# A two-layer decoder step on one core: six more page buffers for values, two places for split weights, gate weights first, another last LayerNorm

## The chip, the cores and the metric

The kernel runs on one core of a Trainium2 chip. The metric is the device time of one execution in microseconds, the median of three runs before: 950.03 us. PE is the matrix engine (TensorE), DVE the vector engine, ACT the scalar engine, POOL GpSimd, and SP the engine whose queue issues nearly all loads.

## The reference

One step for 256 prompt tokens and 64 sample tokens (8 sequences of 8) together, 1024 wide, all in float32. Layer one is a matrix-memory mixer (mLSTM), layer two reads a paged key and value cache: for each sequence 8 pages of 128 tokens of keys, and 8 of values, found through a page table. Both layers have a squared-ReLU MLP of 4096, and each half of a layer ends in a LayerNorm of x * ALPHA + h.

```python
def trunk(x, ...):
    for layer in range(DEPTH):
        if layer < N_A_LAYERS:
            h, state = mlstm_mixer(x, w_in_a[layer], b_gate_a[layer], w_out_a[layer], C0[layer], n0[layer], m0[layer])
        else:
            kv = x @ w_kv
            ctx = kv_side(k, v)
            q = (x @ w_q_b[j]).reshape(B, L, H_B, HD_B)
            h = attend(q, ctx).reshape(B, L, QB_W) @ w_out_b[j]
        x = layer_norm(ALPHA * x + h, ln_g[layer, 0], ln_b[layer, 0])
        x = layer_norm(ALPHA * x + sq_relu_mlp(x, w_up[layer], w_down[layer]), ln_g[layer, 1], ln_b[layer, 1])
```

## The kernel before

All activations lie turned, features on partitions: x is eight chunks of 128 features by 320 tokens. Each dense product is made of tiles of 128 output columns, 192 tiles in 24 groups of eight ("quads": query and key of the mixer, its output gate, its values, its output weights, eight quads of MLP, then the attention's query Q_WQ, keys Q_WK, values Q_WV, output Q_WOB, and eight quads of MLP). To keep float32 accuracy each operand is split into a high and a low part, and a tile is 24 matmuls (eight chunks, three products; lines 528 to 530), some 3.5 us of PE. ACT makes the high part of the weights (`split`, line 1015), DVE the low part (line 1389); both go to four places each, `w_hi` and `w_lo`, tile t to place t % 4, so ACT waits until tile t - 4 is done. Raw weights come in units of two tiles (1 MB) to four buffers; while pages are about, two of these four hold pages.

SP's queue is in order, and its program (lines 420 to 509) is written out by hand: loads of units, of pages, and the waits between them. A wait in it holds everything behind it. `load_page` sends page g to ring buffer g % 8 once page g - 8 has been used (`s_used`); numbers 0 to 63 are keys and 64 to 127 values. `load_unit` waits until both low splits of the unit that was in its buffer are made.

Keys: 32 pairs of pages; PE turns each page (line 845), ACT and DVE copy it, PE forms the scores of a pair (line 887), and between pairs stand the eight tiles of Q_WK and the turning of their results. Values: for two groups of four sequences, 32 pages each (line 939), with one tile of Q_WV before every fourth page of the first group, and the prompt's attention (`p_step`) between those of the second. Then the attention's output is rounded and the output tiles begin.

The start: the sample tokens come in two halves and the gate weights after them on ACT's queue (lines 1029, 1030); seventeen matmuls of zeros (line 561) run before PE turns the eight chunks of x, and the gates' matmuls (`gates`, lines 552 to 554) begin after the sixth chunk. DVE then makes low splits of three tiles and the gates' row chain (lines 1426 to 1447).

The end: after each of the last quad's tiles its chunk of x is final (line 1693), PE turns it back to tokens (`y_turn`), and DVE takes statistics (line 1638) and multiplies by the gain (`y_gained`). After the last, DVE joins the statistics (line 1909), ACT and DVE form 1/std, and DVE makes the result of three groups of tokens (128, 128, 64) by two long operations each (lines 1921, 1923); each group is stored as it is ready.

Of the kernel before, what the change touches and what calls it, by code (L numbers as in the profile page):

```python
# [12 lines left out]
F32 = mybir.dt.float32  # L13
# [6 lines left out]
DM = 1024  # L20
# [22 lines left out]
RAW, SPL = 4, 4  # L43

# [89 lines left out]
def build(nc, x_prompt, x_sample, state_C, state_n, state_m, cache_k, cache_v, page_table,  # L134
# [4 lines left out]
    with ctx:  # L139
# [16 lines left out]
        raw = [put(f"raw{i}", [128, 8, 256]) for i in range(RAW)]  # L156
        WH = [put(f"w_hi{i}", [128, 8, 128], F32R) for i in range(SPL)]
        WL = [put(f"w_lo{i}", [128, 8, 128], F32R) for i in range(SPL)]
# [88 lines left out]
        page = [put(f"page{i}", [128, DM], F32, w_) for i, w_ in enumerate([b_] * 4 + [raw_at] * 4)]  # L247
# [18 lines left out]
        st = put("y_stats", [128, 3, 8, 6], F32, fin_at)  # L266
        mv = put("y_mean_var", [128, 3, 2], F32, fin_at)
        fin = put("y_small", [128, 4, 3], F32, fin_at)
        evc, vc, rsc, nmr = [fin[:, i, :] for i in range(4)]
        QZ = [put("q_padded0", [128, H, 4, 32], F32, b_)]  # L270
# [49 lines left out]
        s_evr, s_evt, s_gbr = sem("eps_row_done"), sem("eps_turned"), sem("gain_bias_rows_in")  # L320
        s_vm, s_aqz, s_cq, s_cqc = [
# [10 lines left out]
        s_in = [sem(f"page_in{i}") for i in range(RING)]  # L332
# [87 lines left out]
        def _(sp):  # L420
# [73 lines left out]
            pages(NPG + 19, NPG + 28)  # L494
            load_unit(4 * Q_WOB + 1)
            pages(NPG + 28, 2 * NPG)
# [1497 lines left out]
```

## Time and profile before

| | us |
|---|---|
| median of three runs | 950.03 (949.31 to 952.37) |
| the profiled execution | 950.97 |
| its span, first to last instruction | 949.2 |
| PE busy | 914.6 (96%) |
| DVE busy | 632.2 (67%) |
| ACT busy | 430.1 (45%) |
| mean granted clock of PE | 0.984 of full |
| HBM read and written | 175.22 MB, 6.32 MB |

A row of the profile gives an engine, the line of the kernel, the operation with its output and input, and times. Idle time stands with what released the engine. In the chain of waits each row is a start, a length and what ran or was waited for, followed back from the last instruction; it is the view that says what a saving would be worth. "Windows" gives the busy time of each engine in a stretch, with the clock that PE was granted.

### The profile page before, as it was taken

How to read it: one execution, taken by the hardware profiler on the slowest of the kernel's cores; microseconds unless marked ns; L12 is line 12 of the kernel's file. 1: busy time of each engine (PE TensorE's matmuls, PEld its weight loads, DVE VectorE, ACT ScalarE, POOL GpSimd, SP SyncE). 2: the span in 40 equal slices, each digit the busy share in tenths (PEclk: the TensorE clock that was granted, in tenths of full speed). 3: DMA queues.
4: the chain of work that ended last, by engine and by line, in shares of the span. 5: the costliest groups of instructions: out<-in, count | busy, mean ns of one | idle time of the engine just before them, and what ended most of it. 6: DMA issues, size and time to landing. Idle time of an engine off the chain costs nothing.

```text
span 949.2 us, 18902 instructions
## 1 busy us (share of the span) xinstructions
PE 914.6 (96%) x7571; PEld 855.8 (90%) x7571; DVE 632.2 (67%) x1117; ACT 430.1 (45%) x806; POOL 56.3 (6%) x69
## 2 busy tenths in 40 slices
PE   8999998999999999999999999989899999999993
PEld 7999977989999999999888778877799999999993
DVE  4667568868887475677576847435468797747556
ACT  3435563457446254445344453333446644526320
POOL 0000006400000000220000000000130000000000
PEclk8999999999999999999999999999899999999997
DMA  9953313654454454465887998999654445554401
GB/s 284 268 172 103 121 45 82 180 167 161 134 166 146 137 171 137 146 246 186 311 280 253 349 360 308 385 391 394 188 174 134 143 142 204 149 161 133 135 1 55
DMA packets 134075, 182.77 MB, mean 193 GB/s; under 512 B 5827, under 2 KB 116107, under 8 KB 133988
## 3 DMA queue, kind: packets, MB, share of 16 engines
q1 hardware_dynamic: 125994, 175.97, 56.1%
q10 hardware_dynamic: 7354, 3.49, 1.4%
q0 software_dynamic: 640, 2.10, 0.8%
q8 instruction: 60, 0.98, 0.4%
q14 instruction: 27, 0.22, 0.1%
HBM read 175.22 MB, written 6.32 MB: 191 GB/s over the span
## 4 chain that ended last, share of the span: by engine, by line
PE 88%; DVE 5%; ACT 2%; DMA 2%; issue 1%; ACTq 1%; SPq 0%; DVEq 0%
PE ps L528 23%; PE ps L530 23%; PE ps L529 23%; PE ps L845 6%; PE ps L887 3%; PE ps L939 2%; DMA page<-in_cache_v_dram 1%; DVE w_lo L1389 1%; DMA wg_raw<-in_w_in_a_dram 1%; PE ps L543 1%; ACTq L1135 0%; PE ps L714 0%; DVE y_tok L1923 0%; ACT probs_turned L1316 0%; PE ps L924 0%
## 5 line engine op out<-in xcount | busy, mean ns | idle before, releaser
L1015 ACT ACTIVATE w_hi<-raw 128x1024 fp32r<-128x1024 f32 x192 | 202.6, 1057 | 251.9 <-PE ps L530 249.4
L1389 DVE TENSOR_TENSOR w_lo<-raw,w_hi 128x1024 fp32r<-128x1024 f32 x192 | 235.1, 1225 | 112.9 <-ACT w_hi L1015 112.6
L528 PE MATMUL ps<-x_hi,w_hi 128*128 128x322 f32 (+1 forms) x888 | 279.8, 315 | 0.4 <-DVE w_lo L1389 0.4
L530 PE MATMUL ps<-x_hi,w_lo 128*128 128x322 f32 (+1 forms) x888 | 276.6, 312 | 0.0
L529 PE MATMUL ps<-x_lo,w_hi 128*128 128x322 f32 (+1 forms) x888 | 276.1, 311 | 0.0
L528 PE MATMUL ps<-h_hi,w_hi 128*128 128x320 f32 x640 | 200.7, 314 | 2.0 <-DVE h_lo L1897 1.1
L529 PE MATMUL ps<-h_lo,w_hi 128*128 128x320 f32 x640 | 199.1, 311 | 0.0
L530 PE MATMUL ps<-h_hi,w_lo 128*128 128x320 f32 x640 | 198.9, 311 | 0.0
L528 PEld LDWEIGHTS ps<-x_hi,w_hi 128*128 128x128 f32 x888 | 168.3, 189 | 6.0 <-ACT k_turned L1282 2.9
L529 PEld LDWEIGHTS ps<-x_lo,w_hi 128*128 128x128 f32 x888 | 168.7, 190 | 0.2
L530 PEld LDWEIGHTS ps<-x_hi,w_lo 128*128 128x128 f32 x888 | 167.6, 189 | 0.0
L528 PEld LDWEIGHTS ps<-h_hi,w_hi 128*128 128x128 f32 x640 | 121.6, 190 | 6.2 <-DVE x L1552 3.4
L529 PEld LDWEIGHTS ps<-h_lo,w_hi 128*128 128x128 f32 x640 | 121.6, 190 | 0.0
L530 PEld LDWEIGHTS ps<-h_hi,w_lo 128*128 128x128 f32 x640 | 121.5, 190 | 0.0
L845 PE MATMUL ps<-base,page 128*128 128x128 f32 x512 | 63.3, 275 | 0.7 <-ACT k_turned L1282 0.7
L845 PEld LDWEIGHTS ps<-base,page 128*128 128x128 f32 x512 | 56.3, 141 | 8.0 <-issue 6.2
L1756 DVE COPY k_turned<-ps 128x512 f32<-128x512 f32 x64 | 43.8, 690 | 24.6 <-PE ps L845 23.4
L1693 DVE TENSOR_TENSOR x<-x,ps 128x320 f32<-128x320 f32 x64 | 31.1, 487 | 42.3 <-PE ps L530 41.2
L1282 ACT ACTIVATE k_turned<-ps 128x512 f32<-128x512 f32 x64 | 36.1, 591 | 28.0 <-PE ps L845 28.0
L1666 DVE SCALAR_TENSOR_TENSOR fm<-ln_neg_mu,ps 128x320 f32<-128x320 f32 x64 | 35.0, 547 | 3.8 <-PE ps L530 3.7
L1668 DVE SCALAR_TENSOR_TENSOR fm<-ln_std,ps,fm 128x320 f32<-128x320 f32 x64 | 35.6, 556 | 2.3
L939 PE MATMUL ps<-page,probs_turned 128*32 128x128 f32 x1024 | 33.4, 275 | 3.6 <-DMA page<-in_cache_v_dram 2.0
(330 smaller groups left out, 884.7 us busy)
## 6 DMA issues: line engine op xcount, KB each, us to landing
raw<-in_w_up_dram SPq DMA_DIRECT2D x32, 1024.0 KB, 5.7
raw<-in_w_down_dram SPq DMA_DIRECT2D x32, 1024.0 KB, 5.3
page<-in_cache_k_dram SPq DMA_DIRECT2D x64, 512.0 KB, 5.2
page<-in_cache_v_dram SPq DMA_DIRECT2D x64, 512.0 KB, 7.2
raw<-in_w_in_a_dram SPq DMA_DIRECT2D x12, 1024.0 KB, 9.2
raw<-in_w_kv_dram SPq DMA_DIRECT2D x8, 1024.0 KB, 6.5
raw<-in_w_out_a_dram SPq DMA_DIRECT2D x4, 1024.0 KB, 5.3
raw<-in_w_q_b_dram SPq DMA_DIRECT2D x4, 1024.0 KB, 5.2
```

Of the source, the lines that this page charges most:

```text
L528: mm(out, WH[t % SPL][:, k, :], hi[:, k, 0:width], start=(k == 0), stop=False)
L529: mm(out, WH[t % SPL][:, k, :], lo[:, k, 0:width], start=False, stop=False)
L530: last = mm(out, WL[t % SPL][:, k, :], hi[:, k, 0:width], start=False, stop=(k == 7))
L845: last = nc.tensor.transpose(bank[:, 128 * j:128 * j + 128], page[P % RING][:, 128 * h:128 * h + 128], ident)
L939: last = mm(o_bank(G, bb)[32 * j:32 * j + 32, c:c + 128], PT[G][:, 8 * a_ + p, 32 * j:32 * j + 32], page[g % RING][:, 128 * h:128 * h + 12 ...
L1015: A(WH[t % SPL][:, :, :], raw[RBUF[u]][:, :, 128 * (t % 2):128 * (t % 2) + 128], ACT.Copy)\
L1282: A(KT[P // 2 % 2][:, 0:4, 128 * (P % 2):128 * (P % 2) + 128], slot_bank(P // 2, 2 * (P % 2))[:, :].rearrange("p (h t) -> p h t", h=4), AC ...
L1389: V.tensor_tensor(WL[t % SPL][:, :, :], raw[RBUF[t // 2]][:, :, 128 * (t % 2):128 * (t % 2) + 128], WH[t % SPL][:, :, :].bitcast(F32), ALU ...
L1666: own(V.scalar_tensor_tensor(f[:, :], nmu[:, :], bank[:, T:T + 1], bank[:, 0:T], ALU.mult, ALU.add))
L1668: V.scalar_tensor_tensor(f[:, :], sd[:, :], bank[:, T + 1:TW], f[:, :], ALU.mult, ALU.add)\
L1693: V.tensor_tensor(X[:, n, :], X[:, n, :], bank[:, 0:T], ALU.add)\
L1756: V.tensor_copy(KT[P // 2 % 2][:, 4:8, 128 * (P % 2):128 * (P % 2) + 128], slot_bank(P // 2, 2 * (P % 2) + 1)[:, :].rearrange("p (h t) -> ...
```

## The change

- Value pages 0 to 5 get buffers of their own, `page8` to `page13`: four in places 2 and 3 of `w_hi` and `w_lo`, one over the squares and sums of the LayerNorm, one over the padded queries of the first group. They are loaded between the key pages. After that all fourteen buffers take values in turn, from value page 50 on only ten.
- While pages are about, split weights of Q_WK and Q_WV have places 0 and 1 only (`PLACE`), and a tile's splits are made after the evacuation of the tile two before, in place of ahead of it. Units and pages change their order in SP's queue, and SP waits there for "all query tiles done", and for pair 15's scores before value page 5.
- The gate weights are issued ahead of the sample tokens on ACT's queue; nineteen warming matmuls, not seventeen. DVE splits tile 3 within the row chain.
- The last LayerNorm: y_turn stands within the next tile, ahead of its fifth chunk; DVE's statistics and gain of a chunk come before the next residual; seven chunks' statistics are joined ahead of the last tile. The sample tokens leave DVE's long operations: ACT makes gained rows of each chunk, PE turns them by a matmul with the identity, and at the end adds (-mean, std) times (gain, bias) to them; ACT scales by 1/std and stores. The second prompt group is finished and stored in two halves.

```diff
+PLACE = [t % 2 if Q_WK <= t // 8 <= Q_WV else t % SPL for t in range(NT)]
+PLACE_BEFORE = [max((w for w in range(t) if PLACE[w] == PLACE[t]), default=-1) for t in range(NT)]
...
+EARLY, LEFT_OUT = 6, 50
+PAGE_AT = [g % RING for g in range(NPG)]
+_turn = [RING + i for i in range(EARLY)] + list(range(RING))
+for _v in range(NPG):
+    if _v == LEFT_OUT:
+        _turn = [b for b in _turn if not RING <= b < RING + 4]
+    PAGE_AT.append(_turn[0])
+    _turn = _turn[1:] + _turn[:1]
+PAGE_BEFORE = [max((w for w in range(g) if PAGE_AT[w] == PAGE_AT[g]), default=-1) for g in range(2 * NPG)]
+PAGE_LOADS = [PAGE_AT[:g + 1].count(PAGE_AT[g]) for g in range(2 * NPG)]
+PLACES_FREE = max(g for g in range(2 * NPG) if RING <= PAGE_AT[g] < RING + 4) + 1
...
-page = [put(f"page{i}", [128, DM], F32, w_) for i, w_ in enumerate([b_] * 4 + [raw_at] * 4)]
+sq_at = [fs_at]
+page = [put(f"page{i}", [128, DM], F32, w_)
+        for i, w_ in enumerate([b_] * 4 + [raw_at] * 4 + [wh_at] * 2 + [wl_at] * 2 + [sq_at])]
...
-        if g >= RING:
-            sp.wait_ge(s_used, g - RING + 1)
-        sp.dma_start(page[g % RING][:, :], cache[bass.ds(number, 1)].rearrange("a t h d -> (a t) (h d)"))\
-            .then_inc(s_in[g % RING], 16)
+        if PAGE_BEFORE[g] >= 0:
+            sp.wait_ge(s_used, PAGE_BEFORE[g] + 1)
+        sp.dma_start(page[PAGE_AT[g]][:, :], cache[bass.ds(number, 1)].rearrange("a t h d -> (a t) (h d)"))\
+            .then_inc(s_in[PAGE_AT[g]], 16)
...
+    sp.wait_ge(s_mm, 8 * Q_WQ + 8)
+    pages(8, 12)
+    load_page(NPG)
+    pages(12, 16)
+    load_page(NPG + 1)
+    pages(16, 18)
     load_unit(4 * Q_WK + 3)
-    pages(8, 22)
+    pages(18, 21)
+    load_page(NPG + 2)
+    pages(21, 24)
+    load_page(NPG + 3)
+    pages(24, 26)
     load_unit(4 * Q_WV)
-    pages(22, 30)
+    pages(26, 30)
+    load_page(NPG + 4)
+    pages(30, 34)
     load_unit(4 * Q_WV + 1)
-    pages(30, 40)
+    pages(34, 37)
+    sp.wait_ge(s_sc, 16)
+    load_page(NPG + 5)
+    pages(37, 42)
     load_unit(4 * Q_WV + 2)
-    pages(40, NPG + 9)
+    pages(42, NPG)
+    pages(NPG + EARLY, NPG + 17)
     load_unit(4 * Q_WV + 3)
-    pages(NPG + 9, NPG + 19)
+    pages(NPG + 17, NPG + 27)
     load_unit(4 * Q_WOB)
-    pages(NPG + 19, NPG + 28)
+    pages(NPG + 27, NPG + 36)
     load_unit(4 * Q_WOB + 1)
-    pages(NPG + 28, 2 * NPG)
+    pages(NPG + 36, 2 * NPG)
...
+        sp.dma_start(gb2[i:i + 1, :], row[1, 1:2, :]).then_inc(s_gbr, 16)
...
+    sp.wait_ge(s_yf, 1)
+    sp.dma_start(y_prompt[0, 0:128, :], Yt[:, 0, :]).then_inc(s_yp, 16)
...
-        sp.wait_ge(s_yf, i + 1)
-        sp.dma_start(y_prompt[0, 128 * i:128 * i + 128, :], Yt[:, i, :]).then_inc(s_yp, 16)
-    sp.wait_ge(s_yp, 16 * 2)
+        sp.wait_ge(s_yf, i + 2)
+        c = slice(512 * i, 512 * i + 512)
+        sp.dma_start(y_prompt[0, 128:256, c], Yt[:, 1, c]).then_inc(s_yp, 16)
+    sp.wait_ge(s_yp, 16 * 3)
...
-    for i in range(17):
+    for i in range(19):
...
-        if n >= 4:
-            pe.wait_ge(s_ty, n - 3)
-        turn3(ps[2 + n % 4], X[:, n, :]).then_inc(s_yt, 1)
+        if n >= 2:
+            pe.wait_ge(s_ty, n - 1)
+        turn3(ps[2 + n % 2], X[:, n, :]).then_inc(s_yt, 1)
+        pe.wait_ge(s_xg, n + 1)
+        mm(ps[4 + n // 4][0:64, 128 * (n % 4):128 * (n % 4) + 128], XG[:, n, :], ident, start=(n % 4 == 0),
+           stop=True, skip_group_check=True)
...
+    def y_between(n, t):
...
+        def ready(k):
+            if k == 4:
+                y_turn(n - 1)
+            return s_lo, t + 1
+        return ready
...
+    def y_sample_centred():
...
+        pe.wait_ge(s_msd, 1)
+        pe.wait_ge(s_ty, 8)
+        nc.tensor.transpose(ps[2][0:2, 0:64], ms[:, :], ident[0:64, 0:64]).then_inc(s_mst, 1)
+        pe.wait_ge(s_msc, 1)
+        pe.wait_ge(s_gbr, 64)
+        for half in range(2):
+            mm(ps[4 + half][0:64, :], msT[:, :], gb2[:, 512 * half:512 * half + 512], start=False, stop=True,
+               skip_group_check=True).then_inc(s_yz, 1)
...
-                    dense(t, HH[g % 2], HL[g % 2])
+                    dense(t, HH[g % 2], HL[g % 2], y_between(n, t) if l == 2 and i == 7 and n >= 1 else None)
...
-                if l == 2 and i == 7 and n >= 1:
-                    y_turn(n - 1)
...
-        if t >= SPL:
-            act.wait_ge(s_mm, t - SPL + 1)
-        A(WH[t % SPL][:, :, :], raw[RBUF[u]][:, :, 128 * (t % 2):128 * (t % 2) + 128], ACT.Copy)\
+        if PLACE_BEFORE[t] >= 0:
+            act.wait_ge(s_mm, PLACE_BEFORE[t] + 1)
+        if t == 8 * Q_WOB + 2:
+            act.wait_ge(s_used, PLACES_FREE)
+        A(WH[PLACE[t]][:, :, :], raw[RBUF[u]][:, :, 128 * (t % 2):128 * (t % 2) + 128], ACT.Copy)\
...
+    act.dma_start(wgraw[:, :, :], lhs_k(win[:, 3072:3088])).then_inc(s_gw, 16)
...
-    act.dma_start(wgraw[:, :, :], lhs_k(win[:, 3072:3088])).then_inc(s_gw, 16)
...
+                    if i == 7 and l == 2:
+                        act.wait_ge(s_xr, 8 * 3 + n + 1)
+                        A(XG[:, n, :], X[:, n, TP:T], ACT.Copy, scale=lnT[:, 24 + n:25 + n]).then_inc(s_xg, 1)
...
-        split_to(t + 4)
+        split_to(min(t + 4, 8 * Q_WK + 1))
...
-        split_to(8 * Q_WV + n + 3)
...
+        split_to(8 * Q_WV + n + 2)
...
-    act.wait_ge(s_yf, 3)
+    act.wait_ge(s_mst, 1)
+    A(msT[:, :], ps[2][0:2, 0:64], ACT.Copy).then_inc(s_msc, 1)
+    for half in range(2):
+        act.wait_ge(s_yz, half + 1)
+        A(Yt[0:64, 2, 512 * half:512 * half + 512], ps[4 + half][0:64, :], ACT.Copy, scale=rsc[0:64, 2:3])\
+            .then_inc(s_yc, 1)
+    act.wait_ge(s_yc, 2)
...
+    split(3)
...
-            ins = V.bn_stats(st[0:w, i, n, :], ps[2 + n % 4][0:w, 128 * i:128 * i + 128])
-        if n == 7:
+            ins = V.bn_stats(st[0:w, i, n, :] if n < 7 else st8[0:w, i, 3:9],
+                             ps[2 + n % 2][0:w, 128 * i:128 * i + 128])
+        if n >= 6:
...
-        bank, c = ps[2 + n % 4], slice(128 * n, 128 * n + 128)
+        bank, c = ps[2 + n % 2], slice(128 * n, 128 * n + 128)
...
-            dve.wait_ge(s_gbr, 32)
+            dve.wait_ge(s_gbr, 64)
...
-                        bcast(gbR[:, 0, c], 1, 2), ALU.mult)
-        V.tensor_tensor(Yt[0:64, 2, c], bank[0:64, 256:384], gbR[0:64, 0, c], ALU.mult).then_inc(s_ty, 1)
+                        bcast(gbR[:, 0, c], 1, 2), ALU.mult).then_inc(s_ty, 1)
...
+    def y_joined():
...
+        for i, w in ((0, 128), (1, 128), (2, 64)):
+            ins = V.bn_aggr(mv[0:w, i, :], st[0:w, i, :, :].rearrange("p n s -> p (n s)"))
+        own(ins)
+        V.tensor_copy(st8[:, :, 1], mv[:, :, 0])
+        V.tensor_scalar(st8[:, :, 2], mv[:, :, 1], 896.0, None, ALU.mult)
...
+                        V.memset(st8[:, :, 0:1], 896.0)
...
+                    if i == 7 and l == 2 and n >= 1:
+                        split_to(t + 3)
+                        y_stats(n - 1)
+                        y_gained(n - 1)
+                        if n == 7:
+                            y_joined()
...
+    split_to(8 * Q_WOB + 3)
...
-        ins = V.bn_aggr(mv[0:w, i, :], st[0:w, i, :, :].rearrange("p n s -> p (n s)"))
+        ins = V.bn_aggr(mv[0:w, i, :], st8[0:w, i, :])
...
+    V.tensor_scalar(ms[:, 0:1], mv[0:64, 2, 0:1], -1.0, None, ALU.mult)
...
+    V.tensor_tensor(ms[:, 1:2], vc[0:64, 2:3], rsc[0:64, 2:3], ALU.mult).then_inc(s_msd, 1)
...
-    for i, w in ((0, 128), (1, 128), (2, 64)):
-        if i == 2:
-            dve.wait_ge(s_yf, 1)
-        own(V.scalar_tensor_tensor(YZ[i % 2][0:w, :], gbR[0:w, 0, :], nmr[0:w, i:i + 1], gbR[0:w, 1, :],
+    for i in range(2):
+        own(V.scalar_tensor_tensor(YZ[i][:, :], gbR[:, 0, :], nmr[:, i:i + 1], gbR[:, 1, :],
...
-        V.scalar_tensor_tensor(Yt[0:w, i, :], Yt[0:w, i, :], rsc[0:w, i:i + 1], YZ[i % 2][0:w, :],
-                               ALU.mult, ALU.add).then_inc(s_yf, 1)
+        for c in ((slice(0, DM),), (slice(0, 512), slice(512, DM)))[i]:
+            V.scalar_tensor_tensor(Yt[:, i, c], Yt[:, i, c], rsc[:, i:i + 1], YZ[i][:, c],
+                                   ALU.mult, ALU.add).then_inc(s_yf, 1)
```

## Rows read from the trace of the kernel before

**Rows 1.** The page: PE busy us, share, count; DMA share in 40 slices

```profile
PE 914.6 (96%) x7571; PEld 855.8 (90%) x7571; DVE 632.2 (67%) x1117; ACT 430.1 (45%) x806; POOL 56.3 (6%) x69
...
DMA  9953313654454454465887998999654445554401
```

**Rows 2.** Chain of waits, 0 to 85 us: start us, us, what

```profile
2.03 7.39 DMA wg_raw<-in_w_in_a_dram
...
12.87 0.27 PE ps L553
...
16.78 0.44 ACT x_hi L1038
...
30.94 0.15 PE ps L529
```

**Rows 3.** DMA issues before 2.1 us: size, us from issue to landing

```profile
x_tok<-in_x_sample_dram ACTq DMA_DIRECT2D x1, 128.0 KB, 3.0
...
x_tok<-in_x_sample_dram ACTq DMA_DIRECT2D x1, 128.0 KB, 4.5
...
wg_raw<-in_w_in_a_dram ACTq DMA_DIRECT2D x1, 64.0 KB, 7.4
```

**Rows 4.** PE's timeline, 9 to 50 us: start, us, operation, [idle before <-releaser]

```profile
11.46 0.61 PE L552 MATMUL ps<-x_hi,wg_hi 128*128 128x320 f32 x1 [1.46 <-DVE wg_lo L1415]
...
30.12 0.39 PE L528 MATMUL ps<-x_hi,w_hi 128*128 128x320 f32 x1 [0.41 <-DVE w_lo L1389]
```

**Rows 5.** Windows: us, busy PE PEld DVE ACT POOL, clock, DMA share, GB/s

```profile
11.50:17.30 5.80, 5.80 (x20) 4.82 (x21) 2.39 (x7) 1.91 (x6) 0.14 (x1) 0.50 1.08 361
```

**Rows 6.** Timeline of DVE, 9 to 40 us

```profile
18.20 3.50 DVE L1389 TENSOR_TENSOR w_lo<-raw,w_hi 128x1024 fp32r<-128x1024 f32 x3
...
24.26 0.48 DVE L1430 SCALAR_TENSOR_TENSOR row<-row,row 8x320 f32<-8x320 f32 x1 [1.04 <-ACT row L1046]
```

**Rows 7.** The chain of waits, 520 to 538 us

```profile
520.21 1.00 PE ps L887 x16
...
528.37 1.75 PE ps L845 x16
...
537.36 1.90 PE ps L845 x16
```

**Rows 8.** DMA view of 525:530, 590:600 and 610:615

```profile
page<-in_cache_k_dram SPq DMA_DIRECT2D x3, 512.0 KB, 4.4
...
DMA packets 1736, 3.63 MB, mean 363 GB/s; under 512 B 92, under 2 KB 1108, under 8 KB 1733
...
page<-in_cache_v_dram SPq DMA_DIRECT2D x5, 512.0 KB, 8.6
```

**Rows 9.** Windows as in rows 5: the keys' end, the values' middle

```profile
530.00:568.00 38.00, 38.00 (x450) 28.53 (x448) 22.70 (x42) 20.23 (x48) 0.00 (x0) 1.00 0.96 354
...
605.00:617.00 12.00, 10.75 (x165) 9.87 (x167) 5.72 (x12) 4.09 (x12) 0.00 (x0) 1.00 1.04 396
```

**Rows 10.** PE's waits, 568 to 674 us: total us, times, longest

```profile
PE ps L939 <- DMA page<-in_cache_v_dram: 2.0, 2, 1.3
```

**Rows 11.** Values, 583 us in the chain of waits, 617 us in PE's timeline

```profile
583.48 1.88 PE ps L939 x64
...
616.89 0.65 PE L939 MATMUL ps<-page,probs_turned 128*32 128x128 f32 x16 [1.25 <-DMA page<-in_cache_v_dram]
```

**Rows 12.** The chain of waits, 700 to 710 us: one 320-column pair

```profile
706.19 0.54 PE ps L750 x2
```

**Rows 13.** Timeline of DVE, 930 to 950 us

```profile
933.64 0.49 DVE L1693 TENSOR_TENSOR x<-x,ps 128x320 f32<-128x320 f32 x1 [2.25 <-PE ps L530]
...
935.88 0.82 DVE L1909 BATCH_NORM_AGGREGATE y_mean_var<-y_stats 128x2 f32<-128x48 f32 x3
...
938.20 1.28 DVE L1921 SCALAR_TENSOR_TENSOR y_rest<-gain_bias_rows,y_small 128x1024 f32<-128x1024 f32 x1
...
944.55 1.28 DVE L1923 SCALAR_TENSOR_TENSOR y_tok<-y_tok,y_small,y_rest 64x1024 f32<-64x1024 f32 x1
```

More of the change, by code:

```diff
@@ L265, in build @@
         gbR = put("gain_bias_rows", [128, 2, DM], F32, gb_at)
-        st = put("y_stats", [128, 3, 8, 6], F32, fin_at)
+        st = put("y_stats", [128, 3, 7, 6], F32, fin_at)
+        st8 = put("y_stats_joined", [128, 3, 9], F32, fin_at)
         mv = put("y_mean_var", [128, 3, 2], F32, fin_at)
         fin = put("y_small", [128, 4, 3], F32, fin_at)
+        XG = put("x_sample_gained", [128, NC8, TS], F32, fin_at)
+        ms = put("y_mean_std", [64, 2], F32, fin_at)
+        msT = put("y_mean_std_rows", [2, 64], F32, fin_at)
+        assert fin_at[0] <= b_[0] + 4096
+        gb2 = put("gain_bias_pair", [2, DM], F32, h1_at)
         evc, vc, rsc, nmr = [fin[:, i, :] for i in range(4)]
+        qz_at = [b_[0]]
+        page.append(put("page13", [128, DM], F32, qz_at))
         QZ = [put("q_padded0", [128, H, 4, 32], F32, b_)]
@@ L320, in build @@
         s_evr, s_evt, s_gbr = sem("eps_row_done"), sem("eps_turned"), sem("gain_bias_rows_in")
+        s_xg, s_msd, s_mst, s_msc, s_yz = [
+            sem(n) for n in ("x_sample_gained", "y_mean_std_done", "y_mean_std_turned", "y_mean_std_copied",
+                             "y_sample_centred")]
+        s_yc = sem("y_sample_done")
         s_vm, s_aqz, s_cq, s_cqc = [
@@ L331, in build @@
             sem(n) for n in ("pS_done", "p_max", "p_exp", "p_norm", "p_turn", "p_turn_copied", "p_out", "p_out_copied")]
-        s_in = [sem(f"page_in{i}") for i in range(RING)]
+        s_in = [sem(f"page_in{i}") for i in range(RING + EARLY)]
         s_used, s_half = sem("page_used"), sem("page_half_turned")
@@ L527, in dense @@
                         pe.wait_ge(*chunk_ready(k))
-                    mm(out, WH[t % SPL][:, k, :], hi[:, k, 0:width], start=(k == 0), stop=False)
-                    mm(out, WH[t % SPL][:, k, :], lo[:, k, 0:width], start=False, stop=False)
-                    last = mm(out, WL[t % SPL][:, k, :], hi[:, k, 0:width], start=False, stop=(k == 7))
+                    mm(out, WH[PLACE[t]][:, k, :], hi[:, k, 0:width], start=(k == 0), stop=False)
+                    mm(out, WH[PLACE[t]][:, k, :], lo[:, k, 0:width], start=False, stop=False)
+                    last = mm(out, WL[PLACE[t]][:, k, :], hi[:, k, 0:width], start=False, stop=(k == 7))
                 last.then_inc(s_mm, 1)
@@ L845, in turn_page @@
                         last = nc.tensor.transpose(bank[:, 128 * j:128 * j + 128],
-                                                   page[P % RING][:, 128 * h:128 * h + 128], ident)
+                                                   page[PAGE_AT[P]][:, 128 * h:128 * h + 128], ident)
                     last.then_inc((s_half, s_used)[half], 1)
@@ L940, in page_values @@
                                   PT[G][:, 8 * a_ + p, 32 * j:32 * j + 32],
-                                  page[g % RING][:, 128 * h:128 * h + 128],
+                                  page[PAGE_AT[g]][:, 128 * h:128 * h + 128],
                                   start=(bb % 2 == 0 and p == 0 and a_ == 0), stop=True, skip_group_check=True)
@@ L998, in _ @@
             y_turn(7)
+            y_sample_centred()
         @block.scalar
@@ L1388, in split @@
                 dve.wait_ge(s_hi, t + 1)
-                V.tensor_tensor(WL[t % SPL][:, :, :], raw[RBUF[t // 2]][:, :, 128 * (t % 2):128 * (t % 2) + 128],
-                                WH[t % SPL][:, :, :].bitcast(F32), ALU.subtract).then_inc(s_lo, 1)
+                V.tensor_tensor(WL[PLACE[t]][:, :, :], raw[RBUF[t // 2]][:, :, 128 * (t % 2):128 * (t % 2) + 128],
+                                WH[PLACE[t]][:, :, :].bitcast(F32), ALU.subtract).then_inc(s_lo, 1)
                 split_upto[0] = t + 1
@@ L1449, in _ @@
             for n in range(8):
-                split(8 * Q_QK + n + 3)
+                split_to(8 * Q_QK + n + 3)
                 if n < 5:
@@ L1701, in mlp @@
                             split_to(t + 4)
-                            if i == 7 and l == 2 and n >= 1:
-                                y_stats(n - 1)
-                                y_gained(n - 1)
             mlp(0, Q_MLP0, 8)
@@ L1872, in _ @@
                 kvq(16 + n)
+                split_to(8 * Q_WV + n + 2)
                 if n == 0:
```

13 lines of the change are left out of this document (7 added, 6 removed).

## The prediction

> **What bounds the kernel now.** I read the page's first two parts, then the chain of waits, then PE's own waits, then the windows of three places. PE is busy 96% of the span, and the chain that ended last lies on PE for 88% of it; the DMA engines are full only at the start and in slices 21 to 29 [rows 1]. So nothing is to be had in the weight tiles as such: a change helps only where PE waits, runs at the low clock, or has ended. There are three such places. (a) The first 17 us: the chain waits 7.39 us for the gate weights, then PE turns and multiplies at a granted clock of 0.50, which is the 1.2 GHz level [rows 2, 5]. (b) The stretch of value pages, 573 to 667 us: PE's wait for pages is only 2.0 us in all, in two pieces [rows 10], though DMA there is full at 396 GB/s [rows 9]. (c) The end: VectorE's chain from the last residual at 933.64 to 945.83 us [rows 13].
>
> **Part (a), the gate weights first.** Before, three transfers stand on ACT's queue: the sample tokens' two halves, landing 3.0 and 4.5 us after their issue at 0.75 and 1.38 us, and then the gate weights, issued at 2.03 and landing 7.4 us later, at 9.42 [rows 2, 3]. ACT waits for them before it rounds x, so the first gate matmul stands at 11.46, and PE has idled since 10.0; its clock then is 0.50 until 17.3 [rows 4, 5]. A gate matmul takes 0.27 us of the chain at the low level, one of the same size 0.15 at the high one [rows 2]. After the second sample half was in (1.38 + 4.5 = 5.9), the weights took 3.5 us more, although they are many small pieces. Issued first, with data flowing from about 2.0 us, they should land between 2.0 + 3.5 = 5.5 and 2.0 + (9.4 - 3.3) = 8.1 us (3.3: issue 2.03 plus the same 1.3 us until data flows). The samples now queue behind them, at 6 to 8.6. I take the early end, because 3.5 us is what the weights took with half of the queue's company gone. The two more warming matmuls end at about 6.45 instead of 5.9 (0.28 each), so PE's turning starts 0.55 us later but runs into the gates with no idle time: six chunks to 10.4 us, gates from 10.4 instead of 11.46, at the high level. The twelve gate matmuls and two chunks between 11.46 and the last x_hi at 16.78 [rows 2] took 5.3 us, and at the high level take 12 x 0.15 + 2 x 0.57 = 2.9. That gives 1.1 + 2.4 = 3.5 us. Everything behind moves with it: the three low splits of 18.20 us [rows 6] start about 3.3 earlier, and their two raw units, issued at 3.37 and 6.43 and 9.3 and 9.2 us on the way, are just there. Splitting tile 3 inside VectorE's 1.04 us gap (it waits for ACT there [rows 6]) costs the row chain some 0.2 us, off PE's path, and takes away PE's 0.41 us wait at 30.12 [rows 4]. I take **-3.5 us**; ends -4.5 and +0.5 (the late end, where PE idles after warming and its clock starts low again).
>
> The Trainium skill, DMA: Bandwidth & Descriptors, section Queues, rings and completion order, says that on each DMA engine one queue's descriptors are consumed in ring order. By that rule the samples can land no earlier than about when the gate weights do, which speaks against this swap; the trace has them in that order (3.75, 5.9, 9.4 us), and the late end of the term is its price.
>
> **Part (b), keys.** Six value pages now go out among the keys, and the split weights of the K and V tiles have two places, not four. A high split must wait for the tile two before, not four: V tiles start 5.9 us apart, and the split weights of tile n+2 are ready 4.1 us after tile n ends, before it is wanted. PE loses nothing there. SP's queue is another matter, since it waits in two new ways. It stands at "pair 15 scored" (521.2 us [rows 7]) before it loads value page 5 and key page 37. Key 37 is then issued at 522.8 (SP issued pages each 1.1 us at 602 to 604) and lands 4.4 us later [rows 8], or 5.7 behind the value page: 527.2 to 528.5; it is read at 529.3, second of the pair at 528.37 [rows 7]. Then SP stands again, for the raw buffer of V's third unit: its release needs V tile 1 split into the one place that K tile 7 holds until 525.0, so about 529.5 to 530. Key 42 leaves at 531.4 behind 1 MB (2.6 us) and lands near 537; it is read at 537.36 [rows 7]. Behind it pages come each 1.3 to 1.45 us and are eaten each 1.45. Slack 0 to 0.5 us: I take **+0.5**, ends 0 and +2.5 (landings of 8.6 us as in the value stretch [rows 8]).
>
> **Part (b), values.** The six pages are a lead of 6 x 0.52 MB / 396 GB/s = 8 us of DMA. But the third place where SP stands eats it: V's fourth unit waits until V tile 3 is split, and that place is held until V tile 1 is done at 583.5 [rows 11]; with VectorE's and ACT's evacuation (1.7), the high (1.05) and low split (1.22) this is 587.6 us, and since SP is in order pages 17 and on wait too. From then 47 pages, 3 units and the stores, 29.1 MB, take 73.5 us at 396 GB/s: done at 590.5 + 73.5 = 664.0. Against PE's need: page 28 lands at 611.7 (it is read at 616.89, held by DMA 1.25 us [rows 11, 10]; without the holds it would be read at 614.6), the last at 664.0 for 664.7 (it was read at 666.7). So both holds go, with little to spare, and the tail (attention output, then dense) is PE's own and follows: **-1.7 us** (2.0 less 0.3 for thin places); ends -2.5 and +6.7, the latter at the 354 GB/s of the keys' end [rows 9]: 82 us.
>
> The same page of the skill, section Bandwidth, gives about 358 GB/s as the limit of one core for HBM transfers. That would make the last page 8 us later than PE wants it; the rows show 396 over 12 us of full load [rows 9], so the measurement decides for me, and 363 over a stretch that is not quite full [rows 8] keeps the chance alive.
>
> The splits of output tiles 2 and 3, now after ACT's last rounding, take 2 x 1.05 on ACT and 2 x 1.22 on VectorE; both end at about 676.6 of the old times, the residual wants VectorE at 678, the tile PE at 681: nothing, hidden under output tiles 0 and 1.
>
> **Part (c), the end.** Added on PE: eight matmuls of 128 columns for the sample rows, two instructions each. Their nearest row is the 320-column pair at 0.54 us [rows 12]: 0.22 each, seven of them before the last tile ends, 1.5 us; the turn of chunk 6, formerly behind the last tile, is now inside it: 0.33. VectorE's early joining of seven chunks (statistics 0.68, gain 0.40, aggregate 0.82, two small ones 0.2) may exceed the rest of the last tile by 0.2. So the last residual comes 2.0 us later. Then: statistics of chunk 7 come right behind its turn, -0.4; three aggregates over 9 elements instead of 48 (0.82 us [rows 13]) -0.5; two small operations +0.2; and of six long operations (1.21 to 1.28 each, 938.20 to 945.83 [rows 13]) four remain, one in halves: -2.5. Sum 2.0 - 0.4 - 0.5 + 0.2 - 2.5 = **-1.2 us**; ends -2.5 and +0.5. The sample rows go round by PE beside this: two products of 512 columns, 0.54 x 512/320 = 0.9 us each [rows 12], 1.8 at the low clock, and ACT's copies, 4.9 us in all from the factors on, as long as VectorE's four; it would be late by at most 0.5.
>
> **The sum.** -3.5 + 0.5 - 1.7 - 1.2 = -5.9 us against the profiled execution, 950.97 us (span 949.2, and 1.8 around it), which is 0.94 above the median of the three timed runs; the same difference off the median 950.03 gives **944.1**.
>
> **The rivals.** *The start gives nothing* (samples land late, PE's clock low again until about 15): then -2.4 in all, **947.6**. For it: the order on ACT's queue [rows 3]; against it: the 3.5 us that the weights took alone. *The lead is worthless*: SP's standing still leaves the two holds where they were and costs a microsecond at keys 37 and 42: -3.5 + 1 + 0 - 1.2, **946.3**. *Slower*: one mechanism, SP standing behind the split weights with only two places, in its two spots. If transfers after each standstill run at 354 GB/s and land after 8.6 us, key 37 and key 42 come 2.5 us late and the last value page 6.7 us late: -3.5 - 1.2 + 2.5 + 6.7 = +4.5, **954.5**. It decides from the point where the last value page lands more than 5 us after 664.7. *More than I think*: start -4.5, tail -2, values -2.5, keys 0: **941.0**.
>
> **How the numbers follow.** Forecast 0.50, no start 0.18, no lead 0.13, more 0.11, slower 0.08. The range leaves out half of the 941.0 case and the slow one, and takes in 947.6 with an upper bound from a half-lost start and late keys: 941.0 to 948.8. About 0.3% (2.85 us) is what a measurement of this kernel can tell from no change: below 947.2 is faster. The forecast, the no-lead and the more case lie there, and a third of the first rival: 0.80; same 0.13; slower 0.07.
>
> **What would show it.** In the changed profile: the first gate matmul near 10.4 at 0.15 us pace and a granted clock near 1 in the window 9 to 17; the sample halves landing by 6.5; PE's first waits on key pages at 37 and 42, under 0.5 us; SP's standstill from about 579 to 588 with DMA idle in it; no wait of PE for value pages; the last residual 2 us later against its tile, and the last VectorE operation 1.2 us earlier against the chain. Wrong if PE waits for value pages by more than 2 us, or if the low clock still covers the gates.

## The result: slower by 2.8%, and the profile after

The changed kernel takes 979.97 us (median of four runs, 978.0 to 983.25) against 951.2 for the one before (four runs, 949.31 to 957.9): a ratio of 1.0282, 95% interval 1.0236 to 1.0327. I had predicted 944.1. The kernel before scatters by itself: its 19 runs beside the first experiments lie between 944.4 and 959.0, so small effects are read below from stages of the profiles as well as from medians.

The page of the kernel after: busy us of each engine, then the granted clock in 40 slices, then the DMA queues (SP's is q1, ACT's q10).

```profile
PE 928.1 (95%) x7594; PEld 859.3 (88%) x7594; DVE 628.8 (64%) x1116; ACT 435.0 (44%) x817; POOL 56.3 (6%) x69
...
PEclk9999999999999999999989999988999999999998
...
q1 hardware_dynamic: 126142, 175.98, 54.4%
q10 hardware_dynamic: 7354, 3.49, 1.3%
```

PE is busy 13.5 us longer with nearly the same instructions [rows 1], because part of them ran at a lower clock, and it stands idle longer as well. To find where, I cut each profile at the same events: first turn of a key page, last score of a cached key, first product of a value page, first residual of the attention output (its dense tile done), last residual, end. All in us; the 3.3 us between keys and values are the same in every kernel and left out.

| profile | keys begin | keys | values, prompt attention | dense tiles | end | span |
|---|---|---|---|---|---|---|
| before | 443.3 | 126.5 | 104.9 | 255.6 | 15.6 | 949.2 |
| after | 437.9 | 148.9 | 114.9 | 259.8 | 13.0 | 977.8 |
| difference | -5.4 | +22.4 | +10.0 | +4.2 | -2.6 | +28.6 |

So the start gave more than forecast, the end about what was forecast, and two stages that I had at +0.5 and -1.7 cost 32 us. Where they lie is in PE's own waits of the kernel after: total us, times, longest.

```profile
PE ps L922 <- DVE k_turned L1859: 12.0, 13, 1.1
PE ps L887 <- DVE p_logit L1846: 9.7, 1, 9.7
...
PE ps L600 <- ACT k_turned L1365: 2.9, 8, 0.4
```

None of the three is among the waits of before at that size (there `p_logit` was 1.5 us, `k_turned` 0.7). None is a wait for a page, either: the value pages' 2.0 us [rows 10] are gone, and key pages cost PE 0.2 us. The first and third line are the keys: PE wants to turn the next page, and its PSUM bank is still being copied out. The windows of the whole key stage (us, then busy time of PE, PEld, DVE, ACT, POOL with counts, clock, DMA share, GB/s), before and after:

```profile
443.30:569.80 126.50, 125.84 (x1274) 100.71 (x1272) 82.60 (x145) 57.49 (x125) 0.00 (x0) 1.00 0.87 303
```

```profile
437.90:586.80 148.90, 133.14 (x1274) 102.86 (x1272) 82.16 (x145) 58.24 (x125) 0.00 (x0) 0.97 0.77 279
```

The same 1274 matmuls, and DVE and ACT have no more to do. PE idles 15.8 us instead of 0.7 (15.1 more) and is busy 7.3 us more, and together that is the 22.4. The 7.3 go with the clock, which is 0.97 on the mean of the stage instead of 1.00 and falls in single stretches with such gaps, for instance in this one:

```profile
494.00:500.00 6.00, 4.93 (x34) 3.24 (x33) 3.65 (x7) 0.96 (x2) 0.00 (x0) 0.72 0.99 355
```

### The profile page after: what moved, and what is told of

Read it like the earlier page. It is cut to its first block, busy times and chain, and to the rows that moved or that the text cites. A ratio compares the mean times of both kernels' runs of the same rounds, so it can differ in the third digit from the quotient of the medians.

```text
span 977.8 us, 18965 instructions
## 1 busy us (share of the span) xinstructions
PE 928.1 (95%) x7594; PEld 859.3 (88%) x7594; DVE 628.8 (64%) x1116; ACT 435.0 (44%) x817; POOL 56.3 (6%) x69
## 4 chain that ended last, share of the span: by engine, by line
PE 86%; DVE 6%; ACT 3%; issue 2%; ACTq 1%; DMA 1%; SPq 0%; DVEq 0%; POOL 0%; POOLq 0%
PE ps L585 23%; PE ps L587 22%; PE ps L586 22%; PE ps L922 4%; PE ps L964 3%; PE ps L1016 2%; ACTq L1215 1%; ACT w_hi L1095 1%; DMA page<-in_cache_k_dram 1%; DVE k_turned L1859 1%; DVE w_lo L1478 1%; PE ps L1001 1%; PE ps L618 1%; DVE kvq L1820 0%; DVE kvq L1819 0%
## 5 line engine op out<-in xcount | busy, mean ns | idle before, releaser
L922 PE MATMUL ps<-base,page 128*128 128x128 f32 x512 | 66.8, 283 | 12.8 <-DVE k_turned L1859 12.0
L922 PEld LDWEIGHTS ps<-base,page 128*128 128x128 f32 x512 | 57.9, 145 | 22.9 <-issue 20.7
L964 PE MATMUL ps<-k_turned,q_padded 128*32 128x256 f32 x512 | 36.0, 402 | 0.0
```

Of the source, the lines that this page charges most:

```text
L922: last = nc.tensor.transpose(bank[:, 128 * j:128 * j + 128], page[PAGE_AT[P]][:, 128 * h:128 * h + 128], ident)
L964: last = mm(ps[SCORE_BANK[2 * a_ + r // 2]][32 * j:32 * j + 32, 256 * (r % 2):256 * (r % 2) + 256], QZ[G][:, 4 * a_ + j, bb, :], KT[pair % ...
```

## Theories

*Mine, after the result.* The key stage pays for the **order on ACT and DVE**. With two places, the splits of tile n+2 cannot stand ahead of the evacuation of tile n, as those of n+3 did, without waiting for that tile's end: they were put behind it, and so ahead of the copies that free PE's banks. The values pay for something near the stores of `v_tok`. *Rivals:* SP's standstills starve PE of key pages; the transfers themselves got slower; two places as such are the cost, in whatever order. The experiments take one edit of the change at a time (the start, the end, the order), and then the stores.

## Experiments

**1. The start alone**, on the kernel before: two warming matmuls more, the gate weights first on ACT's queue, tile 3 split inside the gates' row chain.

```diff
-            for i in range(17):
+            for i in range(19):
...
+            act.dma_start(wgraw[:, :, :], lhs_k(win[:, 3072:3088])).then_inc(s_gw, 16)
             for i in range(2):
...
-            act.dma_start(wgraw[:, :, :], lhs_k(win[:, 3072:3088])).then_inc(s_gw, 16)
...
+            split(3)
             dve.wait_ge(s_gln, 1)
```

> The kernel before with the start of the change alone: gate weights first on ACT's queue, nineteen warming matmuls, tile 3 split within the row chain. The trace after shows the last query tile 5.4 us earlier than before. If that is the start's own and it carries through, this is 5 us faster than before: 944 to 946. Rival: the 5.4 us are given back at the key pages, whose loads are bound elsewhere: under 1 us gained.

Ratio 1.0004 [0.9967, 1.0041] (950.45 us, 10 runs), and not the 944 to 946 that I expected. In its profile the keys begin at 438.6, 4.7 us before those of the kernel before, but the value stage takes 113.2 us instead of 104.9. The gain of that profile is lost again by something else, near 622 us: ACT stands 10.23 us in issuing the stores of `v_tok`, and PE then waits 7.7 us for the prompt's attention. That is a first sign that the stores can go wrong without any of the six pages.

**2. The end alone**: the new last LayerNorm on the kernel before, with the sample rows' part taken through PE by an identity matmul for each tile.

> The kernel before with the new last LayerNorm alone. The trace after has 4.40 us a tile in the last quad where before has 3.85, and 13.0 us behind the last residual where before has 15.6. Theory: the matmul with the identity costs 0.55 us a tile, seven times 0.55 is more than the 2.6 us saved at the end: 1 to 2 us slower than before. Rival, my prediction's step at 0.22 us a matmul: 1.2 us faster.

Ratio 1.0021 [0.998, 1.0063] (951.28, 10 runs): the interval holds both no change and the 1 to 2 us of the expectation. Dense tiles 259.8 us instead of 255.6, end 12.5 instead of 15.6: +4.2 and -3.1. Its start is the old one, yet its keys begin at 439.2: before's own start has two forms. The windows of 11.50 to 17.30 us in this kernel and in the next one (old start too) show them:

```profile
11.50:17.30 5.80, 5.80 (x39) 5.42 (x38) 4.56 (x8) 4.35 (x6) 0.14 (x1) 1.00 1.08 362
```

```profile
11.50:17.30 5.80, 5.80 (x24) 4.86 (x23) 3.18 (x8) 2.76 (x7) 0.14 (x1) 0.56 1.08 361
```

With 1.07 us of idle time before the first gate matmul the clock stayed at 1.00 and PE got through 39 instructions; with 1.57 us it was granted 0.56, and 24 got through. Keys began at 439.2 and 445.0. Of the six profiles with the old start, two were at 1.00 there (experiment 2, and before in experiment 6) and four at 0.50 to 0.56 (before, and experiments 3, 5 and 8). The length of the idle time alone does not decide it. In experiment 5 the clock was low after only 0.75 us of it:

```profile
11.50:17.30 5.80, 5.80 (x23) 4.82 (x23) 2.34 (x6) 2.07 (x4) 0.14 (x1) 0.54 1.08 362
```

**3. The order alone**: the kernel before, with its four places, but the splits behind the evacuation, on ACT and on DVE.

```diff
-                    split_to(8 * Q_WK + n + 3)
                     kvq(8 + n)
+                    split_to(8 * Q_WK + n + 3)
```

> The kernel before, with four places for split weights and its own pages, but in the key pairs the split of the weights stands behind the evacuation of the key tile on ACT and on DVE, not ahead of it. Theory: the order makes the loss, since DVE then waits for ACT's split (ACT evacuates, 0.56, then splits, 1.05) before it copies turned keys, and PE waits for those banks: 15 to 22 us slower. Rival: two places make it, since a split has to wait for the tile two before: no change here, under 1 us.

Ratio 1.0196 [1.0112, 1.0279] (973.52, 4 runs). Keys 147.0 us against 126.5: this swap alone costs 20.5 us where the whole change costs 22.4, with no page moved and no place taken. Its waits of PE are those of after:

```profile
PE ps L845 <- DVE k_turned L1756: 11.1, 12, 1.1
...
PE ps L543 <- ACT k_turned L1282: 2.6, 7, 0.4
```

How it comes about is in the timeline of DVE in the kernel before, and then after, behind the same tile (start, us, operation, idle time before and releaser):

```profile
456.41 0.49 DVE L1717 TENSOR_TENSOR kvq<-kvq,ln_rstd 128x320 f32<-128x320 f32 x1
456.82 1.52 DVE L1756 COPY k_turned<-ps 128x512 f32<-128x512 f32 x2
```

```profile
450.79 0.49 DVE L1820 TENSOR_TENSOR kvq<-kvq,ln_rstd 128x320 f32<-128x320 f32 x1
452.86 1.23 DVE L1478 TENSOR_TENSOR w_lo<-raw,w_hi 128x1024 fp32r<-128x1024 f32 x1 [1.57 <-ACT w_hi L1095]
454.00 1.28 DVE L1859 COPY k_turned<-ps 128x512 f32<-128x512 f32 x2
```

Before, the copy follows the evacuation at once. After, DVE first waits 1.57 us for ACT, then splits for 1.23, and the copy comes 2.8 us later. ACT in the kernel after has the high split ahead of its own copies:

```profile
451.31 0.56 ACT L1319 ACTIVATE k_attn<-kvq,b_times_w 128x320 f32<-128x320 f32 x1 [5.78 <-DVE kvq L1820]
451.78 1.04 ACT L1095 ACTIVATE w_hi<-raw 128x1024 fp32r<-128x1024 f32 x1
452.73 1.06 ACT L1365 ACTIVATE k_turned<-ps 128x512 f32<-128x512 f32 x2
```

And PE pays at the banks (L600 turns the tile's K rows, L922 the next page):

```profile
453.36 0.33 PE L600 MATMUL ps<-base,k_attn 128*128 128x128 f32 x1 [0.37 <-ACT k_turned L1365]
...
454.83 1.94 PE L922 MATMUL ps<-base,page 128*128 128x128 f32 x16 [0.92 <-DVE k_turned L1859]
```

**4. After, with the splits one pair later** (behind `kv_out`, ahead of the odd pair's copies), two places and six pages kept.

```diff
                     kv_out(n)
+                    split_to(8 * Q_WK + n + 2)
                 else:
                     kvq(8 + n)
-                    split_to(8 * Q_WK + n + 2)
```

> The changed kernel with two places and all its pages, but the splits of the key tiles stand one pair later, behind the stores of the turned key tile, where no tile has just ended. If the order makes the loss the key stretch returns from 146.9 to 125 or 127 us and the whole to 958 to 961. Rivals: two places or SP's standing still make it: the key stretch stays above 135 us, the whole above 968.

Ratio 1.012 [1.0056, 1.0185] (964.68, 4 runs). Keys 132.6 instead of 148.9, clock 1.00: 16.3 of the 22.4 are back; I had expected nearly all (keys 125 to 127, the whole 958 to 961). Of the 6.1 left 3.2 are again copies, now at the dense tile's banks (7 waits of up to 0.5 us on ACT's `k_turned`); smaller waits make 2.1, 0.5 of them for key pages, and PE is busy 0.8 longer. Two places, six pages and SP's three standstills are all still in here, so in the key stage they cost 6.1 us at most in this order. Values stay bad, at 116.8: ACT stands 12.14 us at the stores.

**5. Two places in before's order**: the kernel before with the splits of n+2 ahead of the evacuation of n, where those of n+3 stood.

> The kernel before with two places for the split weights of key and value tiles and the unit loads set later in SP's order accordingly; no early pages; the splits stand ahead of the evacuation as in before. Order alone, with four places, took 147.0 us for the keys, before 126.5. Theory: with two places a split can't start before the tile two before has ended, which is when its evacuation is due, so the order of before doesn't save it: DVE waits for ACT's split first and evacuates later: 143 to 150 us. Rival: the order is all: 126 to 129 us.

One execution: 1014.0 us, keys 157.0 and values 137.0; before took 961.06 beside it and beside the single executions of experiments 7 and 8, so only the stages are read from these three. Here the rival is right in its own way: none of the three orders tried with two places (keys 148.9, 132.6 and 157.0) reaches the 126.5 of four. Ahead of the evacuation the split needs a place that PE frees only at the end of the very tile that is to be evacuated, and the evacuation stands behind it on ACT and DVE. PE waits for the evacuations, the first row in the values and the second in the keys:

```profile
PE ps L546 <- ACT fm L1239: 21.8, 8, 3.1
PE ps L848 <- DVE kvq L1720: 17.5, 8, 2.2
```

**6. The stores moved**, in before and in after: the three stores of `v_tok` leave ACT's queue, and SP issues them among the loads of the last MLP (`outs` keeps the count that the end waits for; SP's side is left out here).

```diff
-            for q in range(2):
-                store(p_v[0, 128 * q:128 * q + 128], VT[:, q, :, 0:128])
-            store(s_v_d.rearrange("b t h d -> (b t) h d"), VT[0:64, 2, :, 0:128])
+            outs[0] += 3
```

> The kernel before with the three stores of the new values issued by SP in the last MLP, where its queue has time, in place of by ACT between the values' last copy and the prompt attention. In the traces so far ACT stands at these stores for 4.0, 3.9 and 4.9 us (before, tail alone, order alone) or for 10.2, 12.1 and 12.1 us (start alone, changed kernel, splits one pair later), and PE then waits up to 9.7 us for the prompt attention. Theory: the stores' issue is what makes both the changed kernel's last 8 to 10 us and the spread of the kernel before (944 to 959): PE's 1.5 us wait goes and no run is above 950; median 1.5 to 5 us below before. Rival: the pages' own transfers hold the second half of the values: under 0.5 us.

> The changed kernel with the same three stores moved to SP in the last MLP. Theory: from the first value page to the first output residual it takes 104 to 106 us as in before, not 114.9: the whole 979 becomes 968 to 971. Rival: fourteen pages in flight slow PE's second half by themselves: under 3 us gained.

Before: 0.9973 [0.9951, 0.9995] (948.56, 12 runs; none above 951.1, where the 20 runs of before beside them, median 950.26, reach 956.9). After: 969.78 (4 runs), ratio to before 1.0203 [1.0166, 1.0241] in place of 1.0282. By the medians moving them gave 1.7 us in before and 10.2 in after (7.5 by the two ratios). I had expected no run of the former above 950 (three of the 12 are) and the latter at 968 to 971. The value stage is 101.6 and 102.1 us: 0.5 apart in place of 10.0, and both shorter than the 104.9 of before. So 9.5 of the +10.0 go with these stores. ACT's timeline around them, before and then after (ACTq is the issue of a DMA):

```profile
626.61 4.03 ACTq L1135 DMA_DIRECT2D out_dram<-v_tok  x2
630.69 0.40 ACT L1249 ACTIVATE p_logit<-p_logit,p_stats 128x128 f32<-128x128 f32 x1 [3.98 <-DVE p_stats L1736]
```

```profile
643.37 12.11 ACTq L1215 DMA_DIRECT2D out_dram<-v_tok  x2
655.52 0.40 ACT L1332 ACTIVATE p_logit<-p_logit,p_stats 128x128 f32<-128x128 f32 x1 [12.15 <-issue]
```

Behind the issue stands the first exponential of the prompt attention, and PE waits 9.7 us for what comes of it. In after the chain of waits passes through the last of these issues:

```profile
644.09 11.39 ACTq L1215
```

Behind that the clock is low. After, 643.4 to 655.5 and 656 to 670:

```profile
643.40:655.50 12.10, 4.23 (x88) 3.11 (x88) 1.16 (x3) 0.00 (x0) 0.00 (x0) 0.87 1.04 407
656.00:670.00 14.00, 12.66 (x183) 10.08 (x184) 5.08 (x19) 3.49 (x14) 0.00 (x0) 0.64 0.96 339
```

**7. A ring of eight from value page 14 on**, in the kernel after, to test one reason for the long issue: more pages under way at once than before, so that the stores find fuller queues.

```diff
-    if _v == LEFT_OUT:
-        _turn = [b for b in _turn if not RING <= b < RING + 4]
+    if _v == EARLY + RING:
+        _turn = [b for b in _turn if b < RING]
```

> The changed kernel, with its six early pages, but from value page 14 on only the eight old buffers take pages. ACT stood 12.1 us at the stores in both runs with fourteen buffers, 4 to 10 in those with eight. Theory: the number of page transfers under way sets how long the stores' issue lasts: 4 to 6 us here, and 107 to 110 us from the first value page to the first output residual in place of 114.9. Rival: it does not: 10 to 12 us again. The keys stay at 148 or 149 us.

One execution: 978.66 us, values 116.1, and the issue stood 11.05 us:

```profile
641.03 11.05 ACTq L1215 DMA_DIRECT2D out_dram<-v_tok  x2
```

So fourteen buffers at the time of the stores are not needed for a long issue, and experiment 1 says the same: eight buffers, and 10.23 us. But the profiles do sort by something in the change: with the six early pages ACT stood 12.11 (after), 12.14 (experiment 4) and 11.05 us, and with before's pages 4.03, 4.06, 4.94 and 3.60 (before, experiments 2, 3 and 8), 2.70 for all three stores in experiment 5, and 10.23 once (experiment 1).

**8. The identity matmuls left out** of the kernel of experiment 2. It leaves out the sample rows' x in their last LayerNorm.

> The new last LayerNorm alone, on the kernel before, with the eight matmuls with the identity left out (the sample rows come out wrong: their x is missing; the turns stay in the middle of the tiles). Tail alone took 259.8 us from the first output residual to the last residual, before 255.6. Theory: the identity matmul costs the 0.55 us a tile: 255.6 to 256.2 here. Rival: breaking a tile in two for the turn costs it: 258 to 260 here.

One execution, 948.91 us. Dense tiles 256.1 us instead of 259.8, end 13.1. The matmuls themselves are the cost; that the row of dense matmuls is broken there is not (it was broken before too, by the turns of x). What one costs is in the chain of the kernel after, against 0.15 for each dense matmul around it:

```profile
962.38 0.11 PE ps L602
962.48 0.36 PE ps L831 x2
962.85 0.34 PE ps L585
963.19 0.15 PE ps L586
```

0.36 for the two instructions and 0.34 - 0.15 = 0.19 for the dense matmul behind them: 0.55 us for each of the seven tiles that now hold one; the period from tile to tile grew from 3.85 to 4.40.

**9. Start and stores, and two early pages.** The start's edits with the moved stores; and the same with two value pages loaded ahead, in two buffers whose space is idle by then (the squares' and the padded q's), with four places for the split weights and before's order.

```diff
+PAGE_AT = [g % RING for g in range(NPG)]
+_turn = [RING, RING + 1] + list(range(RING))
+for _v in range(NPG):
+    PAGE_AT.append(_turn[_v % len(_turn)])
...
-            pages(22, 30)
+            pages(22, 26)
+            sp.wait_ge(s_mm, 8 * Q_WQ + 8)
+            load_page(NPG)
+            pages(26, 30)
```

> The kernel before with the start of the change and with the stores moved. Start alone reached its first key page 4.7 us earlier than before, and lost it at the stores (10.2 us). Theory: with the stores gone the start's gain is kept: 943 to 945. The start's gain in the low-clock case is 5 us, in a run where the clock stays high anyway (tail alone reached its keys at 439.2) about 1, so against the moved stores alone it is 1 to 5 us. Rival: the start is given back in another place: same as the moved stores alone.

> Like the run before it, plus two early value pages in the two buffers that cost no split weights (over the LayerNorm's squares and over the padded queries), ten buffers in turn for values; four places for split weights and the order of before. Theory: the keys stay at 126.5 us, PE's 2 us of waits for value pages go, yet PE's own chain hides most of it: 0 to 2 us faster than without. Rival of the change's idea: a lead of two pages, 2.6 us of transfer, is worth its 2 us in full or more.

946.2 us (9 runs, 943.93 to 947.52), ratio 0.9953 [0.9932, 0.9975], a little above the 943 to 945 expected; and **942.81** (6 runs, 941.03 to 945.17), ratio 0.991 [0.9884, 0.9936]. The second beats both kernels. Its keys take 126.6 us, as before, and PE's wait for value pages is 0.3 us in place of 2.0 in before and 2.3 in the first. It is 3.4 us faster than the first by the medians, more than the 0 to 2 that I expected, so the rival (the lead is worth its 2 us or more) came true. The value stages of the two profiles are 103.7 and 102.8 us, and the keys 127.3 and 126.6. The profiled execution of the second was its slowest (945.17), so these profiles can't show where the rest of the 3.4 lies.

## Why the prediction was wrong, step by step

| step | forecast | in the profile | what it was |
|---|---|---|---|
| start | -3.5 | -5.4 | mechanism right, size off (the clock at the old start varies) |
| keys | +0.5 | +22.4 | **failed step** |
| values | -1.7 | +10.0 | lead worth 0.3 at most, and the stores: no term for them |
| end | -1.2 | +1.6 (+4.2 - 2.6) | one term mis-sized |

**The start.** The gate weights landed 2.8 us after their issue at 0.76, at 3.6, not at 5.5: issued first, even these small pieces go quickly. The first gate matmul stood at 10.11 (forecast 10.4) with no idle time ahead, and the clock was 1.00 from 11.50 to 17.30:

```profile
11.50:17.30 5.80, 5.80 (x38) 5.49 (x39) 4.04 (x6) 4.51 (x6) 0.14 (x1) 1.00 1.08 360
```

where before got 20 instructions through at 0.50 [rows 5]. The sample halves landed about 5.7 and 7.5 us into the span, behind the gate weights and later than the 6.5 that I named as a sign. The Trainium skill (DMA: Bandwidth & Descriptors, section Queues, rings and completion order) has the descriptors of one ring consumed in order, and the trace agrees. It cost nothing: PE did not wait for them. Of the 5.4 us, 4.0 are there at the first dense matmul (18.5 for 22.5), 0.4 is the wait at 30.12 that went, and the other 1.0 I have not placed. What I had not seen is that with the old start the clock is low in some executions alone (experiment 2). So the gain is 5 us against a run like the one profiled, and less against the median: 2.4 us between experiments 6 and 9 (948.56 and 946.2).

**The keys, the step that failed:** "the split weights of tile n+2 are ready 4.1 us after tile n ends, before it is wanted. PE loses nothing there." The first sentence is right: no dense tile waited for its weights. The second does not follow from it. I costed the moved split by its own due time, and not by what it was moved ahead of on ACT and DVE: the copies that free PE's PSUM banks. The delay measures 2.8 us a tile: 1.57 of waiting for ACT's split and 1.23 of splitting. Both could have been estimated from the 1.05 and 1.22 us a split in my own working for the values. 8 x 2.8 happens to be 22.4 too, but it is not the sum of what PE lost, which is 15.1 us of idle time and 7.3 of busy time. The swap alone, on the kernel before, costs 20.5 (experiment 3); with the splits one pair later the whole change costs the keys 6.1 (experiment 4). The slack of 0 to 0.5 us on key pages, over which I spent a paragraph, was worth 0.2 us of PE's waits, though the chain of waits passes once through the landing of a key page:

```profile
545.83 9.25 DMA page<-in_cache_k_dram
```

The slow rival that I gave had the right place, the split weights with two places, but the wrong victim, SP. Neither of my two signs of being wrong showed: PE waited for no value page, and the clock over the gates was high. They watched the terms that I had, and not the copies or the stores.

**The values.** SP stood where I said: it issued eleven value pages from 575.80 to 596.7, and then not until V's fourth unit, 8.7 us later (forecast: 9).

```profile
575.80 20.92 SPq L505 DMA_DIRECT2D page<-in_cache_v_dram  x11
605.40 0.39 SPq L460 DMA_DIRECT2D raw<-in_w_kv_dram  x1
```

The holds went too, as forecast, since PE has no wait for value pages. But the stretch from the first value page to the stores is 52.9 us before and 52.6 after. I read it so that the 2.0 us went to the same order again, which no run tests by itself for the values. PE's waits of that stretch in the kernel after:

```profile
PE ps L600 <- ACT fm L1319: 1.3, 2, 0.9
PE ps L986 <- DVE v_tok L1944: 1.1, 1, 1.1
```

The first was 0.4 before, the second nothing: 2.0 more, in place of the 2.0. So the rival "the lead is worthless" came true for this stretch, by another way than its own. Then comes what no step of mine had, a second failed step: I put the time at the stores at nothing, since I took the tail of the stage to be PE's own. From the stores to the first residual it is 62.3 us and not 52.0. ACT stands 8.1 us (12.11 - 4.03) longer in issuing two stores, and the other 2 us go with the low clock behind it. Experiment 6 shows that the issue is on the path, in before too. The upper end of this term was also added up wrongly: the last page 8.7 us later than 664.0 would be 6.0 us behind the old read at 666.7, not 6.7.

**The end.** The sample rows' matmul was priced by its nearest row, 0.22 us [rows 12], and costs 0.55, seven times; with it and with the turn that moved into the stage the dense tiles take 4.2 us more instead of 2.0. The rest came nearly as forecast: -2.6, and -3.1 in experiment 2, against -3.2 for the four terms behind the residual. The aggregate over 9 elements took 0.34 us in place of 0.82 [rows 13]:

```profile
966.69 0.34 DVE y_mean_var L2013 x3
```

The net is +1.6 in the profile, and experiment 2 does not tell it from nothing.

**What stays open.** Why the issue of the same stores takes 4.0 us in one execution and 10 to 12 in another. Neither fourteen buffers (experiment 7) nor the six pages (experiment 1) are needed for a long one, but all three profiles with the six pages have it and one of six without. Moving the stores away removes it without explaining it. The profiles show what goes with it: in before's 4.0 us ACT's queue moved 0.51 MB and had 44% of the engines' time; in after's 12.1 us it moved 0.44 MB with 12%, while SP's had 91. These are queues, packets, MB and share, before (626.6 to 630.6) and after (643.4 to 655.5):

```profile
q1 hardware_dynamic: 257, 0.91, 58.0%
q10 hardware_dynamic: 1008, 0.51, 44.3%
```

```profile
q1 hardware_dynamic: 1231, 4.47, 91.4%
q10 hardware_dynamic: 859, 0.44, 12.0%
```

The Trainium skill (DMA: Bandwidth & Descriptors, section Queues, rings and completion order) says that a DMA engine takes the queues it has work for in turn, a packet each. By the profile's packets, ACT's queue had 3.9 for each of SP's before and 0.7 after. Turns between two queues that both always have work would give one ratio, and no run here shows what made two.

## What to carry to other kernels

When work is moved on an in-order engine, price it twice: by when its result is wanted, and by what stands behind it, above all the copies that free another engine's banks; here the second was about 20 us and the first nothing. A buffer that is taken from a pipeline's depth costs the order in which that pipeline could run, so look for space that is idle (two pages there gave 3.4 us by the medians) before taking places in use. A DMA issue on an engine that also computes belongs away from its critical work while the queues are full; moving these stores gave 1.7 us in one kernel and 7.5 to 10.2 in the other.

## What the runs showed of the hardware that I had not expected

- The issue of the second and third store on ACT's queue (512 and 256 KB) held ACT for 3.6 to 12.1 us while page loads filled the DMA engines (3.60 in experiment 8, 4.03 before, 10.23 in experiment 1, 11.05 in experiment 7, 12.11 after).
- DMA moved 407 GB/s over 12 us of full load on this one core. The Trainium skill (DMA: Bandwidth & Descriptors, section Bandwidth) has about 358 GB/s for a core when both of a pair stream and 425 measured on one alone; the traces of this case lie near the second, and the lateness of 8 us that my prediction worked out from the first did not come: PE waited for no value page.
- With one and the same start the granted clock over the gates was 0.50 to 0.56 in four profiles, after 1.46 to 1.57 us of idle time in three and 0.75 in the fourth, and 1.00 in two, after 1.07 and 1.16 us. In the key stage, with waits of 0.4 to 1.1 us, two or three a tile, its mean was 0.97; in experiment 4, with about one a tile and none above 0.8, it was 1.00.
- 64 KB in small pieces took 7.4 us to land behind two other transfers [rows 3] (6.2 to 7.3 in the other profiles with the old start), and 2.8 to 3.8 as the first of its queue.
